# Which PSUM bank a sum takes at a seam between two stages: the next in turn, or one set by hand

## The chip, the cores and the metric

One NeuronCore of a Trainium2 chip runs the whole program in one launch. The metric is the time of one execution on the device in microseconds; the kernel before has a median of 2316.11 us over three runs.

## The reference

A chain of four transformer layers with a batch of one and 512 positions of width 1024, in fp32. The first two (one "even", one "odd") attend to 256 context positions as well. What matters here is the order of the stages, each of which the kernel names:

```
x, xc = _even_layer(x, xc, ...)   # windowed GQA with sink (A), differential attention (B)
x = _odd_layer(x, xc, ...)        # MLA (M), neighbourhood attention with bias (N)
x = layer_ab(x, c_2, ...)         # RG-LRU and NSA (S), then SwiGLU
x = layer_c(x, c_2, ...)          # sparse attention by an index (D), then SwiGLU
return rmsnorm_2(x, final_norm_2)
```

Each layer begins with an RMSNorm that is scaled and shifted by a modulation (a vector times a 1024 x 3072 or 1024 x 6144 matrix, called "ada" in the kernel), projects h to queries, keys, values and gates, attends, and projects the gated result out.

## The kernel before, in words

The five engines each have a function that writes their instructions in the order in which they run: `tensor` (TensorE), `scalar`, `vector`, `gpsimd` and `sync` (the DMA queue). Nothing reorders them. An engine waits for a counter of another one (`wait_ge`), and each counter goes up by one with an event (`then_inc`). `L86` of a profile's row is the line that issues every matmul, `L91` every transpose, `L96` and `L98` every activation, `L120` every copy; so rows are told apart by their tiles: PS is the PSUM, RING the ring of four weight chunks, H and Hr the normed input, GB, WK, EXQ and X working space in SBUF.

The work goes stage by stage: norm ev, projections A, attention A, projections B, attention B, out projection, norm od, projections M, attention M, projections N, attention N, out projection, and so on through S, the first SwiGLU, D, the second SwiGLU. In a projection, `fm` and `fm_split` (a product with features on the partitions) and `tm` and `tm_split` (positions on the partitions) sum 8 or 24 matmuls into one PSUM bank of 128 x 512 fp32, then VectorE or ScalarE copies the bank out. TensorE does not wait for that copy until it wants the same bank again.

Which bank a sum takes is decided while the program is written, by `next_bank`. `turn["set"]` lists the banks that take part, `turn["at"]` counts on, and the next in the list is used:

```
turn["at"] += 1
b = turn["set"][turn["at"] % len(turn["set"])]
take_bank(b, by)
```

`take_bank` makes TensorE wait for the events that empty bank b (`emptied[b]`), and notes who will empty it now. In projections all eight banks take turns, so that a bank comes back seven sums later. Attention is laid out by hand: the scores of a unit go to banks 0 to 3 (`U["sb"]`), the transposed probabilities to 4 and 5 in turn (`turn["set"] = [4, 5]`), the attended values to 6 or 7 (`U["ob"]`); in A and B bank 7 also takes gates. The end of `attention` (L1118) sets the list back to all eight, and leaves the count where it is. At the start bank 7 holds the first modulation columns (`first_mods`) while sums and transposes of "norm ev" turn through banks 0 to 6, and L1298 sets the list back to eight.

The names that the text uses: `first_turned(f)` transposes and scales x for feature block f, two banks a call, and `("mod_h", "ev", f, 0)` is VectorE's instruction that empties the first of the two. `qa` is the first product of projections A. `gates_m` makes the gates gm 4 to gm 7, the last work before attention M; a gate bank is emptied by ScalarE's tanh and then by a VectorE multiply that reads the bank again. `("o", "M", 15)` is the VectorE multiply that empties the last bank of attention M, `qd` the first product of projections N, `("vd", 1)` the last product of projections N (`tm`, four tiles before attention N), emptied by ScalarE for even tiles and by VectorE for odd ones. `vb` is the same in projections B, `q1` the last of projections D. Before each attention `since` makes TensorE wait for the end of the stage before, its own products among them.

Of the kernel before, what the change touches and what calls it, by code (L numbers as in the profile page):

```python
# [297 lines left out]
def program(nc, A, out_d):  # L298
    ctx = ExitStack()
    with ctx:  # L300
# [49 lines left out]
        def close(signals, stage):  # L350
            for s in signals:
                s.at["end", stage] = s.n
# [83 lines left out]
        def bank(i, a=0, b=512):  # L436
            return PS[:, i * 512 + a:i * 512 + b]
# [12 lines left out]
        def ring_view(i, k):  # L450
            s, n = i % NRING, PLAN[i][2]
            return RING[:, s * 2048:s * 2048 + n].rearrange("p (k n) -> p k n", k=k)
# [346 lines left out]
        def on_act(tag, t, s0):  # L799

            return tag == "q1" or (t + s0 // 512 + (tag == "ki")) % 2 == 0
# [36 lines left out]
        def tensor(pe):  # L838
            emptied = {b: [] for b in range(8)}
            turn = {"at": 0, "set": list(range(8))}  # L840
            cur = Cursor()

            def next_bank(event, by):
# [4 lines that stand above are left out]
                where[event] = b  # L848
                return b

            def take_bank(b, by):
                for s, event in emptied[b]:
                    pe.wait_ge(s, event)
                emptied[b] = by

            def ada(n):
                for _ in range(n):
                    if cur.i == len(ADA_STEPS) or not ada_step():
                        break
# [72 lines left out]
            def chunk_done(i):  # L932
                pe_product.at["chunk", i] = pe_product.n
# [68 lines left out]
            def tm(i, ks_, c0, ncol, tag, by, tiles, src, ready):  # L1002
                W = ring_view(i, ks_)
                pe.wait_ge(ring_in[i % NRING], ("ring", i))
                for t in tiles:
                    b = next_bank(("p", tag, t, 0), by(t))
                    for k in range(ks_):
                        ready(k, 0 if t < 4 else 1)
                        pe.matmul(bank(b, 0, ncol), src(k, t * 128, (t + 1) * 128), W[:, k, c0:c0 + ncol], k == 0,
                                  k == ks_ - 1)  # L1010
                    pe.then_inc(pe_product, ("p", tag, t, 0))

            def copied(tag, t, s0):
                return [(act_value if on_act(tag, t, s0) else dve_value, ("e", tag, t, s0))]
# [13 lines left out]
            def gated(tag, t):  # L1028
                return lambda s0: [(dve_value, ("e", tag, t, s0))]

            def scores(tag, u, U):

                nh = len(U["heads"])
                for h in range(nh):
                    for d in range(U["nb"]):
                        by = (dve_max, ("masked", tag, u, h)) if U["masks"][h] is not None else (act_exp, ("exp", tag, u, h))
                        take_bank(U["sb"][h] + d, [by])
                for z in range(len(U["heads"][0])):
                    for h in range(nh):
                        col, w, pairs = U["heads"][h][z]  # L1040
                        at = U["sb"][h] * 512 + col
                        for j, (l, r) in enumerate(pairs):
                            if l is None and nh == 1:
                                pe.wait_ge(pool_value, ("qz", tag, u))
                                l = QZ_at(u, U["halves"][h])
                            elif l is None:
                                l, r = U["q"][h], half(r, U["halves"][h])
                            pe.matmul(PS[:, at:at + w], l, r, j == 0, j == len(pairs) - 1)
                        if z == len(U["heads"][0]) - 1:
                            pe.then_inc(pe_scores, ("scores", tag, u, h))  # L1050

            def turned(tag, u, U):
                pe.wait_ge(dve_probs, ("probs", tag, u))
                for gi, g in enumerate(U["groups"]):
                    b = next_bank(("flip", tag, u, gi), [(act_value, ("pt", tag, u, gi))])
                    kw = U["pv"][g[0]][2]
                    for j, i in enumerate(g):
                        h, col = U["pv"][i][:2]
                        pe.transpose(bank(b, j * 128, (j + 1) * 128)[0:kw, :], P_at(tag, u, h, col, col + kw), ident)
                    pe.then_inc(pe_flipped, ("flip", tag, u, gi))  # L1060
                    if gi == 1:
                        yield

            def products(tag, u, U):
                blocks, by = U["pv"], {}
                for i, z in enumerate(blocks):
                    by.setdefault(z[0], []).append(i)
                lists = list(by.values())
                order = [i for k in range(max(map(len, lists))) for l in lists for i in l[k:k + 1]]
                if U["first"]:  # L1070
                    take_bank(U["ob"], [])
                begun = set()
                for z, i in enumerate(order):
                    h, col, kw, V, O = blocks[i]
                    pe.wait_ge(act_value, ("pt", tag, u, U["of"][i]))
                    pe.matmul(O, V, PT_at(u, i, 0, 128)[0:kw, :], U["first"] and h not in begun,
                              U["last"] and i == by[h][-1])
                    begun.add(h)
                pe.then_inc(pe_attended, ("attended", tag, u))
                if U["done"]:  # L1080
                    emptied[U["ob"]] = [attended_by(tag, u, U)]
# [16 lines left out]
            def attention(tag, extra=None, behind=None):  # L1098
                units, n, lag = UNITS[tag], len(UNITS[tag]), LAG[tag]
                turn["set"] = [4, 5]  # L1100
                for i in range(n + 6):
                    if i < n:
                        scores(tag, i, units[i])
                    flips = turned(tag, i - lag, units[i - lag]) if 0 <= i - lag < n else iter(())
                    next(flips, None)
                    if extra is not None:
                        extra(i)
                    if 0 <= i - lag - 1 < n:
                        products(tag, i - lag - 1, units[i - lag - 1])
                    for _ in flips:  # L1110
                        pass
                    for t, part in FILL.get(tag, {}).get(i, ()):
                        gate_part(t, part)
                    if i in STEP_TURNS.get(tag, ()):
                        ada(1)
                    if behind is not None:
                        behind(i)
                turn["set"] = list(range(8))  # L1118

            def sum_squares(key, srcs, n, by):  # L1120

# [173 lines left out]
            first_mods(3)  # L1295
            first_turned(6)
            first_turned(7)
            turn["set"] = list(range(8))  # L1298
            close(of_pe, "norm ev")


# [27 lines left out]
            for q, tag in enumerate(("qb", "kb")):  # L1329
                for j in range(2):  # L1330
# [4 lines left out]
                        ada(4)  # L1335
                    chunk_done(i)
            for j in range(2):
                tm(9 + j, 8, 0, 256, ("vb", j), lambda t: copied(("vb", j), t, 0), range(6), Ht, whole)
                if j == 0:
                    ada(4)  # L1340
                chunk_done(9 + j)
# [57 lines left out]
            def gates_m(i, t0):  # L1399
                for m in range(2):  # L1400
                    fm(i, 8, m, "gm", t0 + m, gated("gm", t0 + m), LOC, Ht, h_od)
                    if t0 + m not in (2, 3, 7):
                        ada(3)
                chunk_done(i)
# [23 lines left out]
            tm(i, 1, 512, 512, "vm", lambda t: copied("vm", t, 0), range(6), ckv, ckv_ready)  # L1428
            chunk_done(i)
            for j in range(2):  # L1430
                gates_m(FIRST["od_in2"] + 1 + j, 4 + 2 * j)
            close(of_pe, "proj M")
            since(pe, "proj M")
# [11 lines left out]
                    chunk_done(i)  # L1445
            for j in range(2):
                i = FIRST["od_in2"] + 7 + j
                tm(i, 8, 0, 256, ("vd", j), lambda t: copied(("vd", j), t, 0), range(4 if j else 6), Ht, h_od)
                if j == 0:
                    chunk_done(i)  # L1450
                    ada(4)
# [61 lines left out]
            for j in range(2):  # L1513
# [8 lines left out]
                b = next_bank(("p", "q0", j, 0), copied("q0", j, 0))  # L1522
# [135 lines left out]
            tm_split("l1m", i, 128, 128, "v1", lambda t: [(act_value, ("v1", t))])  # L1658
            chunk_done(i)
            i = FIRST["l1_q1"]  # L1660
            for j in range(4):
                for m in range(2):
                    t = 2 * j + m
                    fm_split("l1m", i + j, m, "q1", t, lambda s0: [(act_value, ("e", "q1", t, 0))])
                chunk_done(i + j)
# [2050 lines left out]
```

## Time and profile before

| | |
|---|---|
| median of 3 runs | 2316.11 us (2316.02 to 2316.85) |
| the profiled execution | 2317.48 us |
| its span on the core | 2315.7 us |
| TensorE busy | 2266.7 us (98%), 11976 matmuls |
| VectorE busy | 1306.6 us (56%) |
| ScalarE busy | 795.1 us (34%) |
| GpSimd busy | 326.6 us (14%) |
| granted TensorE clock, mean | 0.998 of full |

The span is what the profiler sees from the first to the last instruction; the time of the execution is 1.8 us more. A row of the view of waits says who waited for whom, for how long in total, how often, and what the longest was. A row of the timeline gives the start, the duration up to the end of the last instruction merged into it, the engine, the line, the operation and its tiles, and in brackets the idle time of the engine before it and who ended it. The ends of matmuls are modelled: in work without a wait a matmul starts a little before the end that the row ahead of it gives.

### The profile page before, as it was taken

To read this page: it belongs to the slowest core of one execution; us is meant where nothing else is said; L and a number is where in the kernel's file an instruction comes from. 1 tells how busy PE (TensorE), PEld (TensorE's weight loads), DVE (VectorE), ACT (ScalarE), POOL (GpSimd) and SP (SyncE) were. 2 spreads that over 40 slices of the span, in tenths; PEclk is the share of its full clock that TensorE was granted. 3 is DMA by queue.
4 is the path that set the end of the run, shared out by engine and by line. 5 is a ranking of instruction groups with operands and counts; after the bars stand their busy time and mean duration, and the time that the engine had idled before them with its cause. 6 is when DMAs were issued, how large, how long until landed. Compare 5 with 4: busy or idle time off the path is not lost.

```text
span 2315.7 us, 30849 instructions
## 1 busy us (share of the span) xinstructions
PE 2266.7 (98%) x11976; PEld 1727.6 (75%) x11976; DVE 1306.6 (56%) x2919; ACT 795.1 (34%) x1707; POOL 326.6 (14%) x349
## 2 busy tenths in 40 slices
PE   7999999999999999999999999999999999999998
PEld 5866577678546667788876888887878678888886
DVE  3565565754246544758768476665368845443334
ACT  4245102531012203723558132223443643222233
POOL 2200110001000111021100110003543001000154
PEclk9999999999999999999999999999999999999999
DMA  7200331002234373023310245554222103322322
GB/s 314 74 19 19 122 115 64 19 19 64 96 118 128 94 218 99 5 70 107 106 41 2 94 163 185 193 186 142 96 96 73 38 1 118 128 100 94 107 93 80
DMA packets 58270, 225.92 MB, mean 98 GB/s; under 512 B 20478, under 2 KB 21118, under 8 KB 41740
## 3 DMA queue, kind: packets, MB, share of 16 engines
q1 hardware_dynamic: 58124, 223.94, 28.9%
q8 instruction: 95, 1.56, 0.3%
q14 instruction: 51, 0.42, 0.1%
HBM read 221.83 MB, written 2.10 MB: 97 GB/s over the span
## 4 chain that ended last, share of the span: by engine, by line
PE 90%; DVE 4%; POOL 2%; ACT 1%; DMA 1%; issue 1%; SPq 1%; POOLq 0%; ACTq 0%; DVEq 0%
PE PS L86 85%; PE PS L91 5%; POOL WKr L103 1%; DMA GB<-in_ev_ada 1%; DVE WK L108 1%; SPq L162 1%; DVE WK L142 1%; ACT WK L98 1%; ACT WKr L96 0%; DVE SM L135 0%; POOL SM L103 0%; DVE WK L115 0%; ACT WK L96 0%; DVE X L115 0%; DMA RING<-in_l_qi 0%
## 5 line engine op out<-in xcount | busy, mean ns | idle before, releaser
L86 PE MATMUL PS<-Hr,GBr 128*128 128x512 f32 (+1 forms) x1332 | 440.8, 384 | 0.0
L86 PE MATMUL PS<-Hr,RINGr 128*128 128x512 f32 (+1 forms) x1112 | 410.1, 373 | 0.0
L96 ACT ACTIVATE WK<-PS 128x512 f32<-128x512 f32 (+2 forms) x391 | 189.0, 516 | 453.9 <-PE PS L86 276.0
L86 PE MATMUL PS<-H,RING 128*128 128x512 f32 (+1 forms) x928 | 336.4, 515 | 2.7 <-DVE GB L115 2.7
L115 DVE SCALAR_TENSOR_TENSOR ACC<-ADA,SM,ACC 128x256 f32<-128x256 f32 x608 | 291.7, 502 | 40.0 <-DMA ADA<-in_l_mod 21.4
L86 PEld LDWEIGHTS PS<-Hr,GBr 128*128 128x128 f32 x1332 | 247.7, 188 | 51.4 <-issue 3.9
L86 PEld LDWEIGHTS PS<-H,RING 128*128 128x128 f32 x928 | 172.1, 190 | 139.4 <-issue 128.9
L103 DVE TENSOR_TENSOR RINGr<-RING,GBr 128x1024 fp32r<-128x1024 f32 x148 | 183.6, 1278 | 138.3 <-ACT GBr L96 137.8
L86 PE MATMUL PS<-RING,GB 128*128 128x256 f32 x1152 | 251.2, 379 | 0.0
L86 PEld LDWEIGHTS PS<-RING,GB 128*128 128x128 f32 x1152 | 218.1, 190 | 30.4 <-issue 1.3
L86 PEld LDWEIGHTS PS<-Hr,RINGr 128*128 128x128 f32 x1112 | 208.8, 188 | 37.8
L96 ACT ACTIVATE GBr<-RING 128x1024 fp32r<-128x1024 f32 (+1 forms) x154 | 154.2, 1046 | 189.4 <-PE PS L86 189.4
L86 PE MATMUL PS<-GBr,WKr 128*128 128x512 f32 (+1 forms) x664 | 210.9, 388 | 2.5 <-POOL WKr L103 2.5
L86 PE MATMUL PS<-GB 64*128 64x256 f32 (+5 forms) x976 | 173.8, 435 | 4.9 <-DVE SM L142 1.6
L86 PE MATMUL PS<-Xr,GBr 128*128 128x512 f32 (+2 forms) x484 | 175.3, 376 | 0.0
L91 PE MATMUL PS<-CN,WK 128*128 128x128 f32 (+1 forms) x1104 | 162.7, 281 | 11.6 <-DVE WK L108 8.0
L91 PEld LDWEIGHTS PS<-CN,WK 128*128 128x128 f32 (+1 forms) x1104 | 118.1, 140 | 67.6 <-issue 25.7
L86 PE MATMUL PS<-WK,GB 128*64 128x128 f32 (+2 forms) x1856 | 158.1, 280 | 0.5 <-ACT EXQ L96 0.5
L103 POOL TENSOR_TENSOR WKr<-GB,WKr 128x512 fp32r<-128x512 f32 x76 | 108.9, 1433 | 340.2 <-ACT WKr L96 337.3
L86 PEld LDWEIGHTS PS<-GBr,WKr 128*128 128x128 f32 x664 | 125.0, 188 | 33.9 <-issue 7.4
L96 ACT ACTIVATE GB<-PS 128x256 f32<-128x256 f32 (+2 forms) x88 | 43.4, 493 | 303.9 <-PE PS L86 303.6
L86 PEld LDWEIGHTS PS<-WK,GB 128*64 128x64 f32 (+2 forms) x1856 | 126.0, 148 | 21.1 <-issue 20.0
(222 smaller groups left out, 2825.3 us busy)
## 6 DMA issues: line engine op xcount, KB each, us to landing
ADA<-in_l_mod SPq DMA_DIRECT2D x96, 512.0 KB, 3.7
RING<-in_l_gu SPq DMA_DIRECT2D x44, 1024.0 KB, 4.9
RING<-in_l_wd SPq DMA_DIRECT2D x24, 1024.0 KB, 4.9
RING<-in_ev_in SPq DMA_DIRECT2D x13, 1024.0 KB, 5.7
ADA<-in_od_ada SPq DMA_DIRECT2D x24, 512.0 KB, 3.6
RING<-in_od_in SPq DMA_DIRECT2D x11, 1024.0 KB, 6.2
RING<-in_l_in SPq DMA_DIRECT2D x10, 1024.0 KB, 5.0
RING<-in_l_out SPq DMA_DIRECT2D x8, 1024.0 KB, 4.9
```

Of the source, the lines that this page charges most:

```text
L86: self.last = self.eng.matmul(out, lhsT, rhs, start=start, stop=stop, skip_group_check=True)
L91: self.last = self.eng.transpose(out, in_, ident)
L96: self.last = self.eng.activation(out, in_, func, bias=bias, scale=scale)
L98: self.last = self.eng.activation(out, in_, func, bias=bias, scale=scale, accum_out=accum)
L103: self.last = self.eng.tensor_tensor(out, a, b, op)
L108: self.last = self.eng.tensor_scalar(out, a, s1, None, op0)
L115: self.last = self.eng.scalar_tensor_tensor(out=out, in0=a, scalar=s, in1=b, op0=op0, op1=op1)
L142: self.last = self.eng.tensor_tensor_reduce(out, a, b, scale, init, op0, op1, accum)
L162: self.last = self.eng.dma_start(out, in_)
```

## The change

A helper `banks_from(b)` makes all eight banks take turns again, with bank b the next. It stands at the two places that set the list back to eight, and at five new ones:

```
--- before.py
+++ after.py
@@ -848,6 +848,10 @@
+            def banks_from(b):
+
+                turn["set"], turn["at"] = list(range(8)), b - 1
+
@@ -1115,7 +1119,7 @@  (the end of every attention)
-                turn["set"] = list(range(8))
+                banks_from(0)
@@ -1295,7 +1299,7 @@
             first_turned(7)
-            turn["set"] = list(range(8))
+            banks_from(7)
             close(of_pe, "norm ev")
@@ -1335,6 +1339,8 @@
             for j in range(2):
+                if j:
+                    banks_from(2)
                 tm(9 + j, 8, 0, 256, ("vb", j), lambda t: copied(("vb", j), t, 0), range(6), Ht, whole)
@@ -1428,6 +1434,8 @@
             for j in range(2):
+                if j:
+                    banks_from(5)
                 gates_m(FIRST["od_in2"] + 1 + j, 4 + 2 * j)
@@ -1445,6 +1453,8 @@
                 i = FIRST["od_in2"] + 7 + j
+                if j:
+                    banks_from(4)
                 tm(i, 8, 0, 256, ("vd", j), lambda t: copied(("vd", j), t, 0), range(4 if j else 6), Ht, h_od)
@@ -1658,6 +1668,7 @@
             i = FIRST["l1_q1"]
+            banks_from(0)
             for j in range(4):
```

No instruction is added, removed or moved on any engine; what changes is the bank that a sum is written to and read from, and with it the counter that TensorE waits for ahead of some matmuls. The order of TensorE's instructions with their waits shows it. At the seam from projections M to attention M (the row with eight waits before is the first matmul of the scores of unit 0, the row of 8 x 512 ahead of it the sum of gate gm 7):

```order
 L86 MATMUL PS<-H,RING 128x512 x7
-L86 MATMUL PS<-GB 128x512 [waits dve_value,act_value,dve_max,pe_attended,pool_value,pe_flipped,pe_scores,pe_turned,pe_product]
+L86 MATMUL PS<-GB 128x512 [waits pe_attended,pe_flipped,dve_max,pe_scores,pool_value,pe_turned,pe_product]
 L86 MATMUL PS<-GB,EXQ 128x512 [waits pool_value]
 L86 MATMUL PS<-GB 128x256
 L86 MATMUL PS<-GB,EXQ 128x256
-L86 MATMUL PS<-CN,ACC 128x1 [waits dve_mod]
+L86 MATMUL PS<-CN,ACC 128x1 [waits dve_value,dve_mod]
```

The scores no longer wait for VectorE's counter `dve_value`, in which the copy of gate gm 7 counts; the modulation sum behind them (L86 with ACC) does, for the bank of gate gm 6. At the seam from attention M to projections N (the two rows of WK,GB are the last attended values, H,RING 128x512 is qd):

```order
 L86 MATMUL PS<-WK,GB 128x128 [waits act_value]
 L86 MATMUL PS<-WK,GB 128x128
-L86 MATMUL PS<-H,RING 128x512 [waits dve_value,ring_in1]
+L86 MATMUL PS<-H,RING 128x512 [waits act_exp,ring_in1]
 L86 MATMUL PS<-H,RING 128x512 x7
-L86 MATMUL PS<-CN,ACC 128x1 [waits act_exp,dve_mod]
+L86 MATMUL PS<-CN,ACC 128x1 [waits dve_mod]
```

qd waited for VectorE's last multiply of attention M in bank 7; it now waits for the exponentials of unit 15 in bank 0.

## Rows read from the trace of the kernel before

**Rows 1.** The page: share of the span by engine in the chain that ended last.

```profile
PE 90%; DVE 4%; POOL 2%; ACT 1%; DMA 1%; issue 1%; SPq 1%; POOLq 0%; ACTq 0%; DVEq 0%
```

**Rows 2.** Waits of TensorE: its work, who it waited for, us in total, times, longest.

```profile
PE PS L86 <- DMA GB<-in_ev_ada: 14.1, 3, 13.5
PE PS L91 <- DVE WK L108: 8.0, 10, 1.6
PE PS L86 <- DVE GB L115: 4.2, 5, 1.5
...
PE PS L86 <- DVE EXQ L110: 1.8, 1, 1.8
...
PE PS L86 <- DVE GB L120: 0.6, 1, 0.6
```

**Rows 3.** Timeline of TensorE, then of VectorE, around the end of norm ev.

```profile
45.90 1.60 PE L86 MATMUL PS<-WK,X 128*128 128x128 f32 x12 [0.26 <-DVE GB L110]
49.33 0.50 PE L86 MATMUL PS<-Hr,WKr 128*128 128x512 f32 x1 [1.82 <-DVE EXQ L110]
...
44.83 0.17 DVE L115 SCALAR_TENSOR_TENSOR SM<-SM,VC 128x4 f32<-128x4 f32 x1
...
48.47 0.80 DVE L110 TENSOR_SCALAR EXQ<-PS,SM 128x512 f32<-128x512 f32 x1
```

**Rows 4.** Timeline of TensorE and VectorE, projections M to attention M.

```profile
695.79 13.98 PE L86 MATMUL PS<-H,RING 128*128 128x512 f32 x32
711.27 1.10 PE L86 MATMUL PS<-GB 128*128 128x512 f32 x2 [1.50 <-DVE GB L115]
...
710.43 0.69 DVE L115 SCALAR_TENSOR_TENSOR GB<-GB,PS 128x512 f32<-128x512 f32 x1 [2.07 <-ACT GB L96]
714.20 0.96 DVE L137 TENSOR_REDUCE SM<-PS 128x1 f32<-128x768 f32 x1 [3.08 <-PE PS L86]
```

**Rows 5.** Timeline of TensorE and VectorE, attention M to projections N.

```profile
786.76 2.84 PE L86 MATMUL PS<-WK,GB 128*128 128x128 f32 x24
790.48 4.96 PE L86 MATMUL PS<-H,RING 128*128 128x512 f32 x11 [0.88 <-DVE GB L115]
...
789.64 0.69 DVE L115 SCALAR_TENSOR_TENSOR GB<-PS,GB 128x512 f32<-128x512 f32 x1 [1.69 <-PE PS L86]
```

**Rows 6.** Timeline of TensorE and VectorE, projections N to attention N.

```profile
893.73 4.70 PE L86 MATMUL PS<-RING,H 128*128 128x256 f32 x21
899.04 1.56 PE L86 MATMUL PS<-GB 64*128 64x512 f32 x8 [0.61 <-DVE GB L120]
...
898.47 0.42 DVE L120 COPY GB<-PS 128x256 f32<-128x256 f32 x1 [5.97 <-PE PS L86]
```

**Rows 7.** Timeline of TensorE: the same kind of seam in B; work that waits for nothing.

```profile
365.73 5.99 PE L86 MATMUL PS<-RING,H 128*128 128x256 f32 x27
371.77 1.56 PE L86 MATMUL PS<-GB 64*128 64x512 f32 x8
...
25.29 5.60 PE L86 MATMUL PS<-WK,X 128*128 128x128 f32 x48
30.82 1.08 PE L86 MATMUL PS<-GB,EXQ 128*64 128x256 f32 x8
```

**Rows 8.** Busy time by stretch: PE, PEld, DVE, ACT, POOL, granted clock, DMA share, GB/s.

```profile
50.20:53.60 3.40, 3.40 (x10) 2.62 (x9) 2.66 (x3) 2.34 (x4) 1.14 (x2) 0.50 0.07 30
53.60:60.00 6.40, 6.40 (x41) 5.59 (x39) 0.39 (x1) 0.60 (x1) 2.28 (x3) 1.00 0.00 0
```

**Rows 9.** Timeline of TensorE in attention N.

```profile
925.23 0.98 PE L91 MATMUL PS<-CN,WK 128*128 128x128 f32 x7 [1.12 <-DVE WK L108]
```

**Rows 10.** Timeline of VectorE and GpSimd in attention N.

```profile
917.47 1.15 DVE L108 TENSOR_SCALAR WK<-WK,SM 128x768 f32<-128x768 f32 x2
...
922.06 3.11 DVE L108 TENSOR_SCALAR WK<-WK,SM 128x768 f32<-128x768 f32 x2
...
922.33 2.43 POOL L103 TENSOR_TENSOR H<-H,CN 128x960 f32<-128x960 f32 x1 [0.64 <-DMA H<-in_rpb]
```

## The prediction, made before the changed kernel ran

> **What bounds the kernel now.** I read the chain that ended last, then what TensorE waits for, then the timeline around each of those waits, and the granted clock. The chain is TensorE for 90% of the span [rows 1], and the table of times has it busy for 2266.7 of 2315.7 us. So a change that leaves every instruction where it is can only win what TensorE idles, at most 49 us, and 13.5 us of that is one wait for the first weights, ahead of any sum that this change touches [rows 2]. The rest is small waits. Those that a bank can cause are waits for an instruction that empties PSUM, and the list has the kinds at hand: a VectorE scalar_tensor_tensor into GB (4.2 us in 5 waits), a tensor_scalar into EXQ (1.8 us, one wait), a copy into GB (0.6 us, one wait) [rows 2]. The waits for L108, 8.0 us, are waits for probabilities, not for banks: nothing in the change reaches them.
>
> The diff resets the turn at seams between stages, so I looked at each seam, on TensorE and on the engine that it waited for. Four of them hold a bank wait.
>
> **The end of norm ev.** TensorE finishes the last transposes at 45.90 + 1.60 = 47.50 us and starts qa at 49.33, 1.82 us idle, right after VectorE's instruction that ran from 48.47 to 49.27 [rows 3]. By the code, seven banks took turns there, the last transposes took banks 5 and 6, and counted on in the list of eight the next one is bank 5 again: qa waits until the transposes written just before it are read. Now qa takes bank 7, whose reader, the modulation columns, ended at 44.83 + 0.17 = 45.00 us, 2.5 us before TensorE gets there [rows 3]. The h values and the weights of qa are other waits; the first of them are met before 47.5, and the later blocks of h are made by VectorE at a pace that does not depend on this bank. Won: 1.82 us, and 0.07 more, since work without a wait starts by that much ahead of the end of the row before it (30.82 against 25.29 + 5.60 = 30.89) [rows 7]. **1.89 us.**
>
> **Projections M to attention M.** The gate gm 7 ends at 695.79 + 13.98 = 709.77 us; its bank, 3, is one of the first that the scores take, and TensorE idles 1.50 us for tanh and for the multiply that follows it from 710.43 [rows 4]. Now gm 6 and gm 7 lie in banks 5 and 6. The scores' banks 2 and 3 were last emptied by copies of vm, two sums of gates earlier and more. TensorE still waits at this place for its own last product, as it does at every seam of this kind: at the one in B it starts at 371.77 against an end of 371.72 [rows 7], so 0.05 us stays. Won: **1.45 us.** What is late next there is the modulation sum behind the scores, which now waits for gm 6, emptied long before. The scores of unit 0 come 1.45 us earlier, VectorE, idle for 3.08 us until they end [rows 4], starts as much earlier, and the stage moves with them.
>
> **Attention M to projections N.** The last attended values end at 786.76 + 2.84 = 789.60 us in bank 7, and qd is given bank 7, which VectorE empties from 789.64: 0.88 us idle [rows 5]. Now qd takes bank 0, whose scores were read by the exponentials of unit 15, and the probabilities made of them, turned and multiplied since. There is no wait for its own product at this place, so the overlap comes back too; I take the 0.07 of above [rows 7]. Won: **0.95 us.**
>
> **Projections N to attention N.** The fourth tile of vd 1 ends at 893.73 + 4.70 = 898.43 in bank 1, the scores of unit 0 want banks 0 to 3, and TensorE idles 0.61 us for the copy from 898.47 [rows 6]. Now the four tiles lie in banks 4 to 7. Won: 0.61 less the 0.05 that stays, **0.56 us.**
>
> **The other resets.** After A, B, S and D, in vb, and in q1, TensorE has no bank wait at the seam; the seam into B, with 0.05 us, is one of them [rows 7]. They cost or win nothing as long as no bank comes back too soon. For that I went through every wait whose bank changes and set the moment that its reader ended against the moment that TensorE comes: the nearest are the turns of banks 4 and 5 inside attention M, which only change places with each other. Of the banks that really come back sooner, the first tiles of vd 1 are the nearest: bank 5 again behind a modulation sum and one tile, which is 16 matmuls or 4.70 / 21 x 16 = 3.6 us, while the copy takes 0.42 us [rows 6]. No new wait, then; between 0 and the size of the largest one removed, 1.82 us [rows 3], I take 0.
>
> **Does the win last?** TensorE is the bound before and after each seam. All other engines are seen to wait for TensorE behind it, VectorE for 3.08 us in M, 1.69 us at the end of M, 5.97 us in the copies of vd [rows 4 to 6], so they start earlier by as much. No wait for a DMA stands in the list after the first weights, and the ring's loads are started by TensorE's own counters, so they move too. Sum: 1.89 + 1.45 + 0.95 + 0.56 = **4.85 us**.
>
> **The clock.** Right after the wait at 49.33 there is a stretch of 3.4 us with a granted clock of 0.50, the 1.2 GHz level, before and behind it 1.00, 2.4 GHz [rows 8]. Ahead of it TensorE had idled 1.82 us, and 0.26 us before that, with 1.60 us of small transposes between [rows 3]. In the stretch 10 matmuls take 3.40 us, where 41 take 6.40 us behind it [rows 8]; at half the clock 3.4 us do the work of 1.7, so it costs up to 1.7 us. If the idle time ahead of it made the clock fall, the stretch goes with it. Against that: the wait of 1.50 us before attention M was followed by no fall, the mean over the whole span being 0.998. Between 0 and 1.7 us I take 0 for the median, for one reason: the profiled execution took 2317.48 us, 1.37 us more than the median of the runs, about the price of the stretch, so that the usual run may not have it.
>
> **The number.** Against the profiled execution the sum is 2317.48 - 4.85 = 2312.63 us with the stretch still in, 2310.9 without it. Against the median, which is 1.37 us lower, 2316.11 - 4.85 = **2311.26 us**. That is 0.21% less. About 0.2%, 4.6 us, is what a measurement of this kernel can tell from no change, so the forecast stands just beyond that line.
>
> **The rivals.**
> 1. *The clock's stretch is in every run and goes*: 2316.11 - 4.85 - 1.7 = 2309.56 us. For it: the stretch lies directly behind the longest of the four waits [rows 3, 8]. Against it: the 1.37 us.
> 2. *Part of the win is lost behind the seam.* In attention N TensorE waits for VectorE's probabilities, 1.12 us at 925.23 [rows 9], and in A and M there are more such waits (8.0 us in 10) [rows 2]; where VectorE rather than TensorE sets the pace of a stretch, coming earlier only lengthens the next wait. If N's 0.56 and half of M's and A's wins (0.73 + 0.95) go, 2.6 us are left: 2313.5 us. Against it: VectorE is seen idle for TensorE behind each seam [rows 4 to 6].
> 3. *Slower: VectorE and GpSimd fall on each other more often in N.* In attention N GpSimd masks four bias tiles with instructions of some 2.4 us; where the second started, at 922.33, VectorE's pair of tensor_scalars took 3.11 us instead of 1.15 [rows 10], and TensorE waited 1.12 us for it [rows 9]. The start of these instructions hangs on a DMA of the bias (GpSimd waited for it), that of VectorE's on TensorE. If the seam moves the one and not the other, up to three more of them can block VectorE for their whole 2.43 us: 2316.11 - 4.85 + 3 x 2.43 = 2318.5 us. It decides from 4.85 / 3 = 1.6 us lost at each on TensorE's side. Against it: the one collision seen cost TensorE 1.12 us, GpSimd's work in N is itself released by TensorE, and it could as well lose the one it has, for 1.1 us more won.
> 4. *The change does not do it*: TensorE's waits stay because another event of the same counter holds them, say the end of a stage in `since`. Then 2316.1 us. Against it: at the M seam the order shows the wait for `dve_value` gone, and the earlier stages' ends were reached long before.
>
> On the third rival the Trainium skill has a rule, in "SBUF — State Buffer", section "Who interferes with whom": VectorE in a two-port mode and GpSimd share one pair of ports, whoever issues first has it for its whole instruction and the other is blocked. By that rule each of GpSimd's instructions could hold up one of VectorE's for its full length. The trace agrees in the one place where they met.
>
> **Chances.** Forecast (its own range 2310.7 to 2311.9) 0.50; rival 1 0.22; rival 2 0.21; rival 3 0.02; rival 4 0.05. The range leaves out rivals 3 and 4 and the far ends of the others: 2309.3 to 2313.6 us. Faster by over 0.2% means below 2311.48: rival 1 and some 0.75 of the forecast, 0.22 + 0.38 = 0.60. Within 0.2%: the rest of the forecast, rivals 2 and 4, 0.38. Slower by over 0.2%: 0.02, for rival 3 and what I don't see.
>
> **What would show it.** In the profile of the changed kernel TensorE has no wait for the tensor_scalar into EXQ and none for the copy into GB, and the waits for the scalar_tensor_tensor into GB fall from 5 to 3, from 4.2 to 1.8 us. In the timeline qa starts at 47.4 us, the first scores of M 0.05 us behind gm 7, qd without a gap. The windows show whether the stretch at 0.50 is there. The end comes 4.85 us sooner on TensorE, or 6.5 with the clock. The prediction is wrong if the four gaps are gone and the span is not shorter by 4 to 7 us, or if a bank wait of over 0.3 us stands at a new place.

## The result, and the profile after

| | before | after |
|---|---|---|
| median | 2316.82 us (13 executions, 2313.86 to 2319.57) | 2310.82 us (13, 2309.35 to 2312.24) |
| ratio, 95% interval | | 0.9975 (0.9968 to 0.9983) |
| profiled execution, its span | 2317.48, 2315.7 us | 2311.98, 2310.2 us |
| TensorE busy | 2266.7 us | 2265.2 us |

The three runs that the prediction had are among the 13. The change is faster by 0.25%, with an interval of 0.17 to 0.32%; a second set of runs (below) gave 0.9973 (0.9963 to 0.9983), 2316.07 against 2310.45 us. The forecast was 2311.26 us.

What TensorE waited for after the change, in the columns of [rows 2]:

```profile
PE PS L91 <- DVE WK L108: 7.9, 10, 1.6
...
PE PS L86 <- DVE GB L115: 1.9, 3, 0.6
PE PS L86 <- DVE SM L142: 1.6, 4, 0.6
```

The wait for the tensor_scalar into EXQ and the one for the copy into GB are gone from the list; of the five for GB L115 the two long ones are. The timeline of TensorE at the four seams, norm ev first, which answers to [rows 3 to 6]:

```profile
46.06 1.60 PE L86 MATMUL PS<-WK,X 128*128 128x128 f32 x12 [0.26 <-DVE GB L110]
47.42 0.48 PE L86 MATMUL PS<-Hr,WKr 128*128 128x512 f32 x1
...
698.58 9.18 PE L86 MATMUL PS<-H,RING 128*128 128x512 f32 x21
707.82 1.13 PE L86 MATMUL PS<-GB 128*128 128x512 f32 x2
...
783.34 2.84 PE L86 MATMUL PS<-WK,GB 128*128 128x128 f32 x24
786.02 1.45 PE L86 MATMUL PS<-H,RING 128*128 128x512 f32 x3
...
886.83 7.07 PE L86 MATMUL PS<-RING,H 128*128 128x256 f32 x32
893.96 1.34 PE L86 MATMUL PS<-GB 64*128 64x512 f32 x6
```

None of the second rows of a pair has a bracket: no idle time is left. The scores start 0.06 us behind the end of their neighbour (698.58 + 9.18 = 707.76, 886.83 + 7.07 = 893.90), as at the seam in B [rows 7]; qa and qd start 0.24 and 0.16 us ahead of it. VectorE at the M seam:

```profile
708.43 0.69 DVE L115 SCALAR_TENSOR_TENSOR GB<-GB,PS 128x512 f32<-128x512 f32 x1 [2.07 <-ACT GB L96]
710.78 0.96 DVE L137 TENSOR_REDUCE SM<-PS 128x1 f32<-128x768 f32 x1 [1.67 <-PE PS L86]
```

The multiply that TensorE used to wait for now runs beside the scores, and VectorE's own idle time before its first work on them is 1.67 us where it was 3.08 [rows 4].

Since no instruction moves on its engine, the same instruction can be looked up in two traces. This table does it for the first instruction behind each seam, for the first profile of each kernel and for a second pair that was taken later (before, third profile; after, second):

| first instruction | before, after (us) | difference | second pair |
|---|---|---|---|
| last turned block of norm ev | 45.90, 46.06 | +0.16 | +0.85 |
| qa | 49.33, 47.42 | -1.91 | -1.22 |
| 59 us in | 59.0, 55.4 | -3.58 | -1.26 |
| 140 us in | 140.1, 138.1 | -2.01 | -1.26 |
| scores of M | 711.27, 707.82 | -3.45 | -2.71 |
| qd | 790.48, 786.02 | -4.46 | -3.73 |
| scores of N | 899.04, 893.96 | -5.08 | -4.35 |
| 1672 us in | 1672.63, 1667.28 | -5.35 | -4.23 |
| near the end | 2304.9, 2299.4 | -5.49 | -4.24 |

Both pairs give the same steps: **2.07 us at norm ev, 1.44 at M, 1.11 at qd** (from -3.42 and -2.68 just ahead of it; 1.04 us at its first matmul, 0.07 more at its second) **and 0.55 at N** (from -4.53 and -3.80), together 5.17 us. Each step stays; behind 1300 us the first pair drifts by 0.4 us more and the second by 0.1 less, and no bank wait stands there. What differs between the pairs is two things that have nothing to do with the seams: how long TensorE waited for the first weights (the DMA of in_ev_ada), and the stretch at 1.2 GHz in the middle.

The waits for the weights first. The clock's records show full clock from 19.49 us in the first profile of before, from 16.36 in the third. The early rise won almost nothing, for behind it TensorE waits for the DMA. The first profile, then the third:

```profile
13.47 10.08 PE L86 MATMUL PS<-GB,EXQ 128*64 128x256 f32 x64 [13.47 <-DMA GB<-in_ev_ada]
23.48 1.05 PE L86 MATMUL PS<-SM,ACC 128*128 128x2 f32 x8
...
32.35 2.20 PE L86 MATMUL PS<-GB,EXQ 128*64 128x256 f32 x16 [0.45 <-DMA GB<-in_ev_ada]
```

```profile
16.74 3.04 PE L86 MATMUL PS<-GB,EXQ 128*64 128x256 f32 x24
19.97 1.08 PE L86 MATMUL PS<-GB,EXQ 128*64 128x256 f32 x8 [0.19 <-DMA GB<-in_ev_ada]
...
22.53 1.08 PE L86 MATMUL PS<-GB,EXQ 128*64 128x256 f32 x8 [0.19 <-DMA GB<-in_ev_ada]
23.55 1.05 PE L86 MATMUL PS<-SM,ACC 128*128 128x2 f32 x8
```

In all 14 profiles the matmul that starts at 22.96 us in the first of them comes 9.34 to 9.49 us behind the first matmul of all, wherever the clock rose (16.36 to 19.49 us). What moves the start of qa is when the first weights land (the first matmul starts at 13.34 to 14.36 us) and a second group of waits for the same tensor around 33 us: the work from 29.95 to 35.02 us of the first profile took 3.73 to 5.88 us.

The stretch in the middle, by stretch after the change, in the columns of [rows 8]:

```profile
50.20:53.60 3.40, 3.40 (x19) 2.88 (x19) 2.50 (x3) 2.86 (x5) 1.31 (x2) 1.00 0.05 19
126.00:129.40 3.40, 3.40 (x26) 2.74 (x25) 3.26 (x9) 2.09 (x6) 0.00 (x0) 0.50 0.00 0
```

The stretch at 1.2 GHz is not at 50 us any more, which gives 1.67 us between 49 and 59 us (-1.91 to -3.58), and it stands at 126 us instead, which takes 1.57 us back (-3.58 to -2.01).

### The profile page after: what moved, and what is told of

It reads as the page before. It is cut to its first block, busy times and chain, and to the rows that moved or that the text cites. A ratio compares the mean times of both kernels' runs of the same rounds, so it can differ in the third digit from the quotient of the medians.

```text
span 2310.2 us, 30843 instructions
## 1 busy us (share of the span) xinstructions
PE 2265.2 (98%) x11976; PEld 1726.2 (75%) x11976; DVE 1305.9 (57%) x2919; ACT 794.8 (34%) x1707; POOL 326.5 (14%) x349
## 3 DMA queue, kind: packets, MB, share of 16 engines
q8 instruction: 95, 1.56, 0.3%
## 4 chain that ended last, share of the span: by engine, by line
PE 90%; DVE 4%; POOL 2%; ACT 1%; DMA 1%; issue 1%; SPq 1%; POOLq 0%; ACTq 0%; DVEq 0%
PE PS L86 85%; PE PS L91 5%; POOL WKr L103 1%; DMA GB<-in_ev_ada 1%; DVE WK L108 1%; SPq L162 1%; DVE WK L142 1%; ACT WK L98 1%; ACT WKr L96 0%; DVE SM L135 0%; POOL SM L103 0%; DVE WK L115 0%; ACT WK L96 0%; DVE X L115 0%; DVE X L103 0%
## 5 line engine op out<-in xcount | busy, mean ns | idle before, releaser
L86 PE MATMUL PS<-Hr,GBr 128*128 128x512 f32 (+1 forms) x1332 | 440.7, 384 | 0.0
L86 PE MATMUL PS<-Hr,RINGr 128*128 128x512 f32 (+1 forms) x1112 | 409.5, 373 | 0.0
L86 PE MATMUL PS<-H,RING 128*128 128x512 f32 (+1 forms) x928 | 336.5, 515 | 1.9 <-DVE GB L115 1.9
L115 DVE SCALAR_TENSOR_TENSOR ACC<-ADA,SM,ACC 128x256 f32<-128x256 f32 x608 | 291.3, 502 | 39.5 <-DMA ADA<-in_l_mod 21.4
L86 PEld LDWEIGHTS PS<-Hr,GBr 128*128 128x128 f32 x1332 | 247.6, 188 | 51.1 <-issue 3.9
L86 PEld LDWEIGHTS PS<-H,RING 128*128 128x128 f32 x928 | 172.2, 190 | 138.6 <-issue 128.2
L86 PE MATMUL PS<-RING,GB 128*128 128x256 f32 x1152 | 251.2, 379 | 0.0
L86 PEld LDWEIGHTS PS<-RING,GB 128*128 128x128 f32 x1152 | 218.1, 190 | 30.4 <-issue 1.3
L86 PEld LDWEIGHTS PS<-Hr,RINGr 128*128 128x128 f32 x1112 | 208.4, 187 | 37.8
L86 PE MATMUL PS<-GBr,WKr 128*128 128x512 f32 (+1 forms) x664 | 210.1, 387 | 2.5 <-POOL WKr L103 2.5
L86 PE MATMUL PS<-GB 64*128 64x256 f32 (+5 forms) x976 | 173.9, 435 | 2.9 <-DVE SM L142 1.6
L86 PE MATMUL PS<-Xr,GBr 128*128 128x512 f32 (+2 forms) x484 | 175.3, 376 | 0.0
L91 PEld LDWEIGHTS PS<-CN,WK 128*128 128x128 f32 (+1 forms) x1104 | 118.3, 140 | 67.4 <-issue 25.7
L86 PE MATMUL PS<-WK,GB 128*64 128x128 f32 (+2 forms) x1856 | 159.2, 281 | 0.5 <-ACT EXQ L96 0.5
L86 PEld LDWEIGHTS PS<-GBr,WKr 128*128 128x128 f32 x664 | 124.6, 188 | 33.9 <-issue 8.1
L86 PEld LDWEIGHTS PS<-WK,GB 128*64 128x64 f32 (+2 forms) x1856 | 126.9, 149 | 21.3 <-issue 20.2
```

The lines of the kernel that those rows point to most:

```text
L86: self.last = self.eng.matmul(out, lhsT, rhs, start=start, stop=stop, skip_group_check=True)
L91: self.last = self.eng.transpose(out, in_, ident)
L115: self.last = self.eng.scalar_tensor_tensor(out=out, in0=a, scalar=s, in1=b, op0=op0, op1=op1)
```

## The experiments

Two questions. Does each reset win what its seam idled, and nothing else? And what is the stretch at 1.2 GHz? The first theory: a reset also shifts the turn for every later seam up to the next reset, so a reset alone can bring up a wait elsewhere, and the set is what keeps them all away. Its rival is the prediction's sum, in which each seam stands for itself. All differences below are of the starts of the same instructions, as above; single times depend on the stretch and on the waits for the first weights as well. On the chip of the first four kernels one run of before took 2317.64 us, on that of the next four its median was 2317.30 us.

**The reset at norm ev alone.** Before, with one edit:

```
-            turn["set"] = list(range(8))
+            banks_from(7)          # end of norm ev
```

> The kernel before with one of the resets alone, banks_from(7) at the end of norm ev. Theory one (a reset takes away the wait at its own seam and, since the count runs on, moves the turn for every seam behind it): qa starts without the 1.82 us, and the seam into attention B, free before, gets a wait for the copy of the last vb tile, 0.47 + 0.13 = 0.6 us; the other three waits stay (1.50, 0.88, 0.61). Span 1.9 - 0.6 = 1.3 us under the kernel before, give or take a stretch of half clock (1.6 us). Theory two (seams are independent): 1.9 us won and no new wait at the seam into B.

2314.76 us, span 2313.0. qa comes 2.07 us sooner against the row ahead of it, as in the whole change. But at 369.32 us, at the seam into attention B where before had no wait, there is a new one:

```profile
365.74 2.97 PE L86 MATMUL PS<-RING,H 128*128 128x256 f32 x13
369.32 1.56 PE L86 MATMUL PS<-GB 64*128 64x512 f32 x8 [0.61 <-DVE GB L120]
```

It takes 0.55 us back, for good. This profile had no stretch at 1.2 GHz. Theory one holds: in before, this seam was free of a wait because of where the count happened to stand.

**The gates of M alone.** Before, with `banks_from(5)` ahead of the second pair of gates.

> The kernel before with banks_from(5) ahead of the gates gm 6 and gm 7 alone. Theory one (the turn moves for all seams behind): the 1.50 us ahead of attention M goes, and the waits of qd (0.88) and of attention N (0.61) go too although nothing was done at their seams; behind attention N the out projection, free before, now waits for VectorE's last multiply of N, about 0.9 us. TensorE wins 1.45 + 0.95 + 0.56 - 0.95 = 2.0 us. Theory two (each seam by itself): 1.45 us won, 0.88 and 0.61 stay.

2315.40 us, span 2313.6. This one reset takes away three waits: 1.44 us at M, 1.11 at qd and 0.55 at N. (The profile had two stretches at 1.2 GHz, at 25.5 and 127.9 us, which the time holds as well.) The shifted turn happens to give qd and the tiles of vd 1 banks that had been free for long. At the out projection behind N the bill comes, 0.85 us:

```profile
979.31 1.84 PE L86 MATMUL PS<-WK,GB 128*64 128x128 f32 x24
981.94 2.42 PE L86 MATMUL PS<-RING,GB 128*128 128x256 f32 x10 [0.78 <-DVE GB L115]
```

**The last tiles of vd alone.** Before, with `banks_from(4)` ahead of vd 1.

> The kernel before with banks_from(4) ahead of the second half of vd alone. Theory one (the turn moves for all seams behind): the 0.61 us ahead of attention N goes, and behind attention S the out projection gets a wait for the last multiply of S, 0.9 us, so that TensorE ends some 0.35 us later than in the kernel before. Theory two: 0.56 us won, nothing new.

2318.02 us, span 2316.2. The N seam wins its 0.55 us, and the out projection behind S loses 0.87:

```profile
1269.64 1.97 PE L86 MATMUL PS<-WK,GB 128*64 128x128 f32 x32
1272.40 1.78 PE L86 MATMUL PS<-RING,GB 128*128 128x256 f32 x7 [0.79 <-DVE GB L120]
```

By its seams alone this reset makes the kernel slower, by 0.3 us. (Its profile had a stretch at 128.1 us.)

**The reset at norm ev undone.** The changed kernel with that one line taken back.

> The changed kernel with the reset at the end of norm ev taken back (all eight banks in turn, the count left). Theory (the four wins add up, and the end of attention A resets the count): qa waits 1.8 us for bank 5 again, the other three waits stay away, TensorE ends 1.9 us later than in the changed kernel, apart from the half-speed stretch, which I expect either at some 50 us, as in the kernel before, or near 126 us, as in the changed one, but not in both. Rival (part of the first win is lost again inside attention A, where TensorE waits for probabilities): less than 1 us later.

2313.56 us, span 2311.8. qa is 2.07 us later than in the changed kernel, and up to attention N nothing else differs at any seam: the reset at the end of attention A cuts the shift off. In attention N it then gains 0.73 us, which the section on the third rival explains. TensorE idled 1.8 us ahead of qa as in before, but the stretch at 1.2 GHz was not behind it; it ran from 127.3 us:

```profile
126.00:129.40 3.40, 2.17 (x12) 1.84 (x14) 3.33 (x7) 1.82 (x7) 0.00 (x0) 0.69 0.00 0
```

**The ends of the attentions alone.** Before, with `banks_from(0)` where `attention` ends.

> The kernel before with banks_from(0) at the end of each attention alone. Theory: of the four waits only that of qd (0.88 us) goes; the wait of attention N (0.61 us) stays with bank 2 in place of bank 1, those of norm ev (1.82) and attention M (1.50) stay. TensorE ends 0.95 us earlier. Rival: a reset at every attention moves so many banks that a new wait of over 0.3 us turns up at some seam.

2313.65 us, span 2311.9. The waits of TensorE:

```profile
PE PS L86 <- DVE GB L115: 3.4, 4, 1.5
...
PE PS L86 <- DVE EXQ L110: 1.8, 1, 1.8
...
PE PS L86 <- DVE GB L120: 0.6, 1, 0.6
```

Only qd's is gone, for 1.11 us. The time is nearly 3.7 us below before's all the same. Against the first profile of before, 0.93 us were won ahead of 46 us, where TensorE waited less for the weights, 1.65 us because this profile had no stretch in the middle, and 1.11 at qd. So two executions of like kernels differ by as much as half of the whole change, and a single time is no evidence on a seam.

**Without the resets in vb and q1.** The changed kernel less those two.

> The changed kernel without the resets in vb and q1. Theory: both only hold a place that the count reaches well there anyway, so TensorE's waits are those of the changed kernel, to 0.1 us, and the span differs by no more than the half-speed stretch (0 or 1.6 us). Rival: they guard a seam: then a wait of 0.3 to 0.9 us stands at the seam into attention B or D.

2310.65 us, span 2308.9. Against the second profile of the changed kernel it is 0.30 to 0.33 us late at every seam from norm ev to 1690 us, and had that before the first reset: the two do nothing for the time as the kernel stands. (They would matter if a stage ahead of them got another number of sums; no run shows that.)

**The two idle spells of attention A filled.** In both kernels TensorE waits in attention A for probabilities; here they are in the run above:

```profile
120.24 1.09 PE L91 MATMUL PS<-CN,WK 128*128 128x128 f32 x8 [1.03 <-DVE WK L108]
...
125.20 1.09 PE L91 MATMUL PS<-CN,WK 128*128 128x128 f32 x8 [1.62 <-DVE WK L108]
```

If these make the clock fall at 126 us, matmuls that nobody reads, put into them, should keep it up. The changed kernel, with

```
+                    for _ in range({4: 2, 5: 3}.get(i, 0) if tag == "A" else 0):
+                        pe.matmul(bank(7), ident, CN[:, C_COS:C_COS + 512], True, True)
```

> The changed kernel with five matmuls of 128x512 added that nobody reads (two in the turn of attention A in which TensorE waits 1.03 us for probabilities, three in the next with 1.63 us). Theory (the half-speed stretch at 126 us comes from these two spells of idle time and nothing else in the kernel): the two waits shrink to under 0.4 us each, there is no stretch at half clock between 60 us and the end of the work, and TensorE ends 1.5 us earlier than in the changed kernel. Rival (the stretch comes by the clock's own beat, whatever TensorE does): it stands somewhere after 60 us all the same, and nothing is won.

2310.28 us, span 2308.5. There was no stretch, but the other half of the expectation failed:

```profile
118.70 1.98 PE L86 MATMUL PS<-CN 128*128 128x512 f32 x4
120.52 1.04 PE L91 MATMUL PS<-CN,WK 128*128 128x128 f32 x8
...
123.73 2.84 PE L86 MATMUL PS<-CN 128*128 128x512 f32 x6
126.41 1.04 PE L91 MATMUL PS<-CN,WK 128*128 128x128 f32 x8
```

The trace records two matmuls for each one written, and 10 of them take 1.98 + 2.84 us, nearly twice the 1.03 + 1.62 us that they were to fill. Behind them TensorE is 1.59 us later than in the second profile of the changed kernel. That is as much as the stretch costs where it comes. In attention N 1.2 us of it came back in this profile, since the wait for VectorE's probabilities, 1.12 us there, was 0.16 us here; the section on the third rival has that wait.

**All together, with more banks chosen by hand.** The run above, and two more places: the tiles of v0 in attention S go to bank 7, the four of va in attention A to banks 7 and 6 in turn, instead of to the turning banks 4 and 5.

```
+                    kept = dict(turn)
+                    turn["set"] = [7]          # S; in A: [7 - t % 2], tile by tile
...
+                    turn.update(kept)
```

> The changed kernel, the five idle-time matmuls of the run before, and fixed banks inside two attentions as well: the tiles of v0 in attention S go to bank 7 instead of taking a turn in banks 4 and 5, the last tiles of va in attention A to banks 7 and 6. Theory: in the changed kernel's profile these turns cost 0.51 us (the turned probabilities wait for v0 1), 0.62 us (v0 3 waits for turned probabilities) and 0.25 us (va 2); all three go, 1.4 us, plus 1.5 us for the clock where the stretch would have come: span some 2.9 us under the changed kernel's 2310.2, 0.3 to 0.4% faster than the kernel before. Rival: the probabilities' own pace takes the 1.4 us back (less than 0.5 us left).

2309.70 us median (6 executions, 2309.19 to 2310.44), ratio to before 0.9969 (0.9957 to 0.9981), span 2308.0. Against the profile with the filled spells alone the new banks win 0.51 us at 109 us, and 1.56 in attention S (at 1174 and 1181 us): 2.07 us, where 1.4 was expected. But in attention N this profile has the wait of 1.12 us that the other was spared, and loses 1.20 us by it. The fillers take another 1.59, as before.

**The same kernels again.** By now the stretch had stood at 50 us, near 127 us, at 25 us, or nowhere, and the waits ahead of it did not tell which. If the execution rather than the kernel decides, the same kernel must show it in different places. Before twice more, the changed kernel and the last version once more, the last two with more times on one chip.

> The kernel before, unchanged, for a second profile. Theory (the stretch at 1.2 GHz is a matter of the execution: in the profiles so far it stood at 50 us, near 127 us, at 25 us as well, or nowhere, with TensorE's waits ahead of it the same): TensorE idles 1.8 us ahead of qa as in the first profile, but the 3.4 us stretch need not be at 50.2 us; it may stand near 127 us or be absent, and the time is then 2316 to 2316.5 us against 2317.5 with one. Rival (the kernel's waits set it): it is at 50.2 us again, and the time is 2317 to 2318 us.

> The kernel before, unchanged, for a third profile. Theory of the execution: of the three profiles of this kernel at least one has the stretch elsewhere or not at all. Rival: all three have it at 50.2 us. In both, the waits of TensorE are the same to 0.2 us.

2317.36 and 2314.35 us. By stretch, the second profile of before, then the third:

```profile
22.30:25.70 3.40, 3.27 (x29) 2.42 (x26) 0.00 (x0) 0.60 (x1) 0.00 (x0) 1.00 0.65 248
25.80:29.10 3.30, 3.30 (x17) 3.30 (x17) 1.46 (x7) 0.66 (x2) 0.00 (x0) 0.50 0.66 263
...
50.20:53.60 3.40, 3.40 (x16) 2.75 (x15) 2.33 (x4) 2.93 (x5) 1.73 (x2) 1.00 0.06 25
...
128.20:131.50 3.30, 3.30 (x26) 2.97 (x26) 3.23 (x7) 1.62 (x4) 0.00 (x0) 0.50 0.00 0
```

```profile
25.80:29.10 3.30, 3.30 (x32) 3.30 (x31) 2.47 (x7) 2.04 (x5) 0.51 (x1) 1.00 0.76 302
50.20:53.60 3.40, 3.40 (x17) 2.81 (x16) 2.36 (x2) 1.14 (x2) 0.25 (x1) 1.00 0.04 14
...
128.20:131.50 3.30, 3.30 (x13) 1.47 (x10) 2.42 (x9) 1.39 (x6) 0.00 (x0) 1.00 0.01 2
```

One file, three profiles: a stretch at 50.2 us; two, at 25.8 and 128.2; none. And the wait ahead of qa was there in both, in the second profile and in the third:

```profile
49.90 0.50 PE L86 MATMUL PS<-Hr,WKr 128*128 128x512 f32 x1 [1.83 <-DVE EXQ L110]
```

```profile
48.12 0.50 PE L86 MATMUL PS<-Hr,WKr 128*128 128x512 f32 x1 [1.83 <-DVE EXQ L110]
```

The rival, that a kernel's waits alone set the stretch, has fallen. What they have to do with it all the same is shown in the last section.

> The changed kernel, unchanged, for a second profile and more times on the chip of the next kernel. Theory of the execution: the stretch near 126 us is there or not, by the execution; times fall into two groups 1.5 us apart, near 2311.7 with it and 2310.3 without. Against before: 5 to 6.5 us less, ratio 0.9972 to 0.9978. Rival (the waits set it): the stretch is at 126 us again and the times lie around one value.

> The version with the two idle spells of attention A filled and the tiles of v0 and va in banks 7 and 6, beside the changed kernel on the same chip. If this version is better than the change: median 1 to 1.5 us below it (0.7 us for the banks, the rest for the executions in which the changed kernel has the stretch). Rival (what it wins at the banks is given back in attention N, where its profile showed a wait 0.85 us longer than that of the version without them): within 0.5 us of it.

The changed kernel: 2310.45 us median (9 executions, 2308.51 to 2311.91), no stretch in its second profile, where the first had one at 126 us. The times don't fall into two clear groups as expected. A spread of other sources lies over them: in the 14 profiles the last turned block of norm ev alone starts at 44.69 to 46.64 us, by the waits for the weights and the stretch at 25.5 us where it came. The last version: 2310.18 us (6 executions), 0.3 us below the change, which is its rival's side ("within 0.5 us"). The rival's reason, a longer wait in attention N, did not recur in this profile: N gave 0.9 us back here, and against the second profile of the changed kernel it is ahead by 1.3 us from norm ev to the end. The fillers eat most of what the banks win. Over both sets it has 2309.9 us in 12 executions against 2310.7 in 22. The version that the numbers point to, the change with the new banks of v0 and va and without fillers, was not run; from the starts it should be 2.07 us below the change, and that is an estimate which leaves out what attention N makes of the shift (it gave or took 0.7 to 1.2 us between profiles).

## Why the prediction came out right, and where it was wrong

**The four seams.** The terms were 1.89, 1.45, 0.95 and 0.56 us, 4.85 in all; measured 2.07, 1.44, 1.11 and 0.55, 5.17 in all, the same to 0.02 us in two pairs of traces. The cause is shown and not only argued: e1, e5, e6 and e2 bring each of them alone, e3 takes one back. Two terms were a little small, for one reason: an instruction that waits for nothing starts further ahead of the modelled end than the 0.07 us of [rows 7]: 0.24 us at qa, 0.16 at qd, and behind qd's first matmul, which took 0.07 us longer after the wait, the second gains that too.

**The number.** 2311.26 us against 2310.82 is nearer than the working deserves. The forecast stood on a median of three, 2316.11 us, and the median of 13 is 2316.82, 0.71 higher; and the two medians lie 6.0 us apart where it had 4.85. The two misses partly cancel, which is luck. Of the 1.15 us between 6.0 and 4.85, the seams explain 0.32. The second set, at 5.6, has only half of the rest, and no run says where it lies.

**"The other resets cost or win nothing."** True of the set, and wrong as a picture of how it works. I took each wait for a property of its seam. The runs show the banks at a seam as the sum of all turns since the last reset: one reset at the gates clears three seams and spoils a fourth (e5), one at norm ev spoils the seam into B (e1), one at vd costs more than it wins (e6). The resets at the ends of the attentions, which win one seam themselves, are what keeps 0.55, 0.85 and 0.87 us from being given back. In this kernel only those of vb and q1 do nothing (e4).

**Does the win last?** Yes: behind each seam the difference stays, -2.01 us from 140 to 709 us, -5.08 from 899 to 1271. Rival 2, that part of it is lost in stretches that VectorE paces, fell. The waits for L108 are as they were, 7.9 us in 10.

**Rival 3, VectorE and GpSimd in attention N.** It didn't happen, but its mechanism is real, and it is the execution that moves it. VectorE's pair of tensor_scalars and GpSimd's masking instruction in the third and in the second profile of before:

```profile
919.24 3.12 DVE L108 TENSOR_SCALAR WK<-WK,SM 128x768 f32<-128x768 f32 x2
```

```profile
919.68 2.26 POOL L103 TENSOR_TENSOR H<-H,CN 128x960 f32<-128x960 f32 x1 [1.10 <-DMA H<-in_rpb]
```

```profile
922.70 1.15 DVE L108 TENSOR_SCALAR WK<-WK,SM 128x768 f32<-128x768 f32 x2
927.26 2.64 DVE L108 TENSOR_SCALAR WK<-WK,SM 128x768 f32<-128x768 f32 x2
```

```profile
926.74 2.23 POOL L103 TENSOR_TENSOR H<-H,CN 128x960 f32<-128x960 f32 x1 [0.80 <-DMA H<-in_rpb]
```

They collide at one pair or at the next, and TensorE ends up 0.7 us apart, with the kernel unchanged. So the expectation that TensorE's waits would be the same to 0.2 us in all profiles of before failed here: 7.2 us in 9 waits for L108 in the second, 8.0 and 7.9 in 10 in the others. In the first profiles of before and after it was the same pair, so that the comparison was spared it.

**The clock.** This is the step that was wrong. I took 0 of 0 to 1.7 us, since the profiled execution lay 1.37 us above the median "so that the usual run may not have it", and made rival 1 of the case that every run has it and loses it. Neither is so. In 14 profiles the mean granted clock, given to three places, was 0.999 in the eight without a stretch and 0.998 or less in the six with one or two. By that mark 12 of the 28 executions of before for which it was recorded were without one, and 12 of 22 of the changed kernel: about half of either. The number came out near because the stretch falls largely out of the difference of medians, not because the usual run lacks it. Among the executions at 0.999 the medians are 2315.5 and 2310.35 us, 5.15 us apart, where the seams give 5.17; at 0.998 and less they are 2317.5 and 2311.2. Whether the changed kernel has a little less of it, at the 6.0 us between the first medians, the spread doesn't let one say: the second set has 5.6.

What does make the stretch is partly open. It came at 50 us once, directly behind 1.8 us of idle time, near 127 us five times, directly behind the spells of 1.03 and 1.62 us, and at 25.5 and 25.8 us once each, with next to no idle time ahead. With the two spells filled it did not come in three profiles out of three, where without fillers it came near 127 us in five of eleven, which is a hint and no proof: of the 12 executions of the last version five have a mean clock of 0.998, and a mean does not say where or why the clock was low. So "if the idle time ahead of it made the clock fall, the stretch goes with it" was half of the story; the last section has the other half.

## What to carry to other kernels

A ring of banks (or of any buffers) that is counted on through a program is coupled from end to end: whether a seam waits depends on how many turns every stage ahead of it took. So fix the count at the start of each stage rather than at the one that waits, test the resets together as well as alone, and look in the list of waits for new ones far behind the edit. Where single executions differ by more than the effect, compare the start of the same instruction in two traces, step by step; here that gave 0.02 us where the times of one kernel spread over 3 to 6. Then look at what else moves the start, as the waits for the first weights did here.

## What the runs showed of the hardware that was not expected

TensorE fell to 1.2 GHz for 3.4 us while it was nearly never idle: in the second profile of before it was busy for 3.27 of the 3.40 us ahead of 25.7 us, and the clock fell there all the same; in the third profile it had been busy for 3.21 of them, and the same transposes ran at 2.4 GHz. The stretch near 127 us stood the same distance behind the moment of the first rise each time, whatever the waits did in between: from 16.76 us to 125.99, from 18.06 to 127.29, from 18.67 to 127.90, from 18.91 to 128.14 and from 18.93 to 128.16.

And whether it came went with where the idle spell of 1.62 us lay. In these five profiles the spell had ended 0.06 to 0.60 us before that moment. Here is its end in the second profile of before, where the clock fell at 128.16 us, and in the first, where the same distance behind the first rise gives 128.72 us, inside the spell, and the clock did not fall:

```profile
127.96 1.82 PE L91 MATMUL PS<-CN,WK 128*128 128x128 f32 x8 [1.63 <-DVE WK L108]
```

```profile
128.98 1.09 PE L91 MATMUL PS<-CN,WK 128*128 128x128 f32 x8 [1.62 <-DVE WK L108]
```

Of the six profiles without fillers and without this stretch, four had the moment inside the spell, as here, and two had it 2.7 and 3.0 us behind its end. At 50 us it is the same: the fall came 30.72 us behind the first rise and 0.88 us behind the end of the 1.82 us wait ahead of qa, and in the other six profiles that have this wait, 30.72 us behind the rise lay inside it, and nothing fell. So the waits of a kernel make a fall possible, and the start of the execution decides whether it comes. That is what these fourteen profiles show without an exception; no run moved a spell on purpose to test it, and the two falls at 25.5 and 25.8 us (both 6.83 us behind the first rise) it does not explain.

The Trainium skill, "TensorE: Matmul & The Clock Gate", section "What's actually happening", says as much of the start: what the hardware watches runs freely and does not begin with the kernel, so that the same kernel warms up at different points. The rises at 16.36 to 19.49 us agree with it, though they spread over 3.1 us where the page gives 500 ns either way; that the start of an execution decides on falls in the middle as well is what these runs add.

The Trainium skill's advice in "Perfetto Trace Analysis", section "Matmuls", is to let independent groups of matmuls rotate through the banks, so that emptying one overlaps with filling the next. This kernel did, and still idled 4.8 us at four seams, since where two layouts of the banks meet the next in turn can be the one just filled.
